# Decay rows by way of memory: turned decay blocks on VectorE instead of TensorE in a one-core hybrid-mixer kernel

## The chip, the cores and the metric

The kernel runs on one core of a Trainium2 chip. The metric is device time in microseconds (us), the median of several executions. Engines are written as the profile writes them: PE is TensorE (PEld its weight load), DVE is VectorE, ACT is ScalarE, POOL is GpSimd and SP is SyncE.

## The reference, cut to what matters

Two blocks run one after the other on 256 tokens of width 2048. The change lies in the first one, in its gated delta rule of 8 heads of width 128:

```python
g = jnp.cumsum(g.reshape(B, H, N, C), axis=-1)
kb = k * beta[..., None]
decay = jnp.exp(jnp.where(incl, g[..., :, None] - g[..., None, :], NEG_INF))
L = jnp.where(strict, jnp.einsum('bhnid,bhnjd->bhnij', kb, k) * decay, 0.0)
T = lax.linalg.triangular_solve(L + eye, jnp.broadcast_to(eye, L.shape), left_side=True, lower=True)
...
intra = jnp.where(incl, jnp.einsum('bhnid,bhnjd->bhnij', q, k) * decay, 0.0)
```

Everything else that fills the time is the dense part around it: `h @ w_in` with more than 12,000 columns, two branch products, `@ w_out`, and the same kind of products of the second block.

## The kernel before, in words

**Pieces.** All dense products are cut into 400 pieces, numbered by ticks 0 to 399. A piece is a 512 KB slab of weights (2 x 128 rows by 512 columns, or 4 x 128 rows by 256 columns). SP loads it into one of five raw buffers (L781), ACT rounds it into a high part `hi_w` (L1002, `split`), DVE computes the remainder `lo_w` (L1406), and PE multiplies with both parts (L2084, L2086, L2094). The split of piece n+2 stands in tick n in the streams of ACT and DVE. There are four split buffers, so ACT may start the high part of piece n as soon as PE has used piece n-4. SP may load into a raw buffer as soon as the low part of the piece five before is done.

**The plan.** `plan()` writes out by hand at which tick every small step stands. Every engine runs through the same list of ticks in order and takes out the steps that are its own. A step that waits for something therefore holds up all that follows it on its engine, the weight splits on ACT and DVE among them. On PE the steps of a tick follow the products of that tick.

**The decay blocks.** Heads are taken in two quads (h = 0, 1) and tokens in two tiles (t = 0, 1). For each of the four (h, t), starting at ticks 65, 69, 73 and 77:

- `gu` (DVE, L1565) multiplies the upper triangle of ones by the log decays, in a high and a low part.
- `gram` (PE): two products with a matrix of ones (L2168) sum these, so that every partition holds the running sum of the decays as a row. Then 8 + 8 products (L2172) form k k^T and k q^T in `aux` banks 1 and 2.
- `decay` (ACT, L1133 and L1136) waits for `gram`, takes the absolute difference of row and column sums, and the exponential.
- `tri` (DVE, L1571 to L1579) masks the decay block below and above the diagonal (`low_m`, `low_t`), forms `attn_t`, and the block `wide` = k k^T times the key factor `k_low` times `low_m`.
- `tri_flip`: PE transposes `wide` (four transposes; in the trace they stand under the helper's line L1973) and ACT copies the result to `low_t` (L1140). The joining steps at ticks 110 to 121 need `low_t`.
- `blocks_away` (POOL, L890) writes the 32x32 diagonal blocks of `wide` to memory for `solve` at tick 83.

`k_scale` on POOL computes `k_low`, `v_shift` on POOL (L900, L901) copies v rows shifted by one to three tokens for the convolution, and `v_tap` on DVE (L1535) reads them. `z_out` on ACT is L1163. POOL's transfers share one queue. `ones_r` (ACT, L1051) makes a rounded copy of the matrix of ones for L2168.

Of the kernel before, what the change touches and what calls it, by code (L numbers as in the profile page):

```python
# [16 lines left out]
F32 = mybir.dt.float32  # L17
F32R = mybir.dt.float32r
# [4 lines left out]
P = 128  # L23
# [183 lines left out]
def plan():  # L207
    steps = [[] for _ in range(TICKS + LAST)]

    def at(tick, *step):  # L210
        steps[tick].append(step)
# [12 lines left out]
    at(18, "ones_r")  # L224
    for n, step in enumerate(("ba", "softplus", "gates", "gcum", "exp_gcum")):
        at(END[("conv", "v", 0, 0)] + 1 + n, step)
    for h in range(2):
        at(conv_end("k", h) + (13, 8)[h], "k_scale", h)

# [21 lines left out]
    for h in range(2):  # L251
        for t in range(NT):
            s = base + 4 * (NT * h + t)
            at(s, "gu", h, t)
            at(s + 1, "gram", h, t)
            at(s + 2, "decay", h, t)
            at(s + 3, "tri", h, t)
            at(s + 5, "tri_flip", h, t)
            at(s + 5, "blocks_away", h, t)
# [181 lines left out]
def build(nc, known, ins, out):  # L441

    ctx = ExitStack()
    with ctx:
# [39 lines left out]
        g_hi = place("g_hi", [P, NT * HEADS], F32R)  # L484
        ones_r = place("ones_r", [P, P], F32R)
# [17 lines left out]
        g_lo = bit(NT * HEADS)  # L503
# [14 lines left out]
        def arena(name, shape, dtype, kb):  # L518
# [14 lines left out]
                  for i, n in enumerate(("low_m", "inv", "wide"))} for t in range(NT)]  # L533
        gu_hi, gu_lo = ([arena(f"gu_{n}{t}", [P, QUAD, P], F32R, 48 + 8 * t + kb) for t in range(NT)]
                        for n, kb in (("hi", 4), ("lo", 2)))
# [36 lines left out]
        for i in range(2):  # L572
# [30 lines left out]
                         for n in ("block", "solved")]  # L603
        scratch = nc.dram_tensor("x2_scratch", [SEQ, D], F32, kind="Internal").ap()
# [31 lines left out]
        v_shifted = {j: signal(f"v_shifted{j}", 16) for j in range(1, CONV)}  # L636
        solved_out = signal("solved_out", 16)
# [205 lines left out]
        def _(pool):  # L843
# [48 lines left out]

            def v_shift(h):

                pool.wait_ge(*act_did.after("v_raw", h, 1))
                pool.wait_ge(*pool_did.after("v_zero", CONV - 1))
                for j in range(1, CONV):
                    if h:
                        pool.wait_ge(*dve_did.after("v_tap", 0, 6))
                    pool.dma_start(v_late[j][j:P], v_late[0][0:P - j]).then_inc(*v_shifted[j].event(h, 0))  # L900
                    pool.dma_start(v_late[j][0:j, 1], v_late[0][P - j:P, 0]).then_inc(*v_shifted[j].event(h, 1))  # L901
# [72 lines left out]
            def tail_(t):  # L974
# [4 lines left out]
                     "solve": solve, "v_shift": v_shift, "inv_zero": inv_zero,  # L979
                     "norm1": norm1, "norm2": norm2, "y_last": y_last, "residual": residual, "att": att, "tail": tail_}  # L980
# [7 lines left out]
        def _(act):  # L988
# [61 lines left out]
            def ones_r_():  # L1050
                act.activation(ones_r[:], ones[:], ACT.Copy).then_inc(*act_did.event("ones_r"))  # L1051

# [26 lines left out]
            def m_out(part, h, s):  # L1079
                c = END[("moba", part, h, s)]  # L1080
                act.wait_ge(*used.after(c))
                if (part, h, s) == ("q", 0, 0):
                    act.wait_ge(*dve_did.after("v_tap", 1, 6))
                act.activation(m_t[part][:, two(h, s)], pairs_of(c)[:, :, 1], ACT.Copy).then_inc(
                    *act_did.event("half", "moba", part, h, s))
# [290 lines left out]
            steps = {"x_flip": x_flip, "sq1": sq1, "ones_r": ones_r_, "softplus": softplus, "exp_gcum": exp_gcum, "sq2": sq2, "split": split, "y_last": y_last, "h2_hi": h2_hi, "h2_rows": h2_rows,  # L1376
                     "raw_out": raw_out, "m_out": m_out, "conv": conv, "conv_silu": conv_silu, "v_raw": v_raw, "v_silu": v_silu,
                     "token_out": token_out, "decay": decay, "tri_flip": tri_flip,
# [15 lines left out]
        def _(dve):  # L1394
# [42 lines left out]
            def gates():  # L1437

                dve.wait_ge(*act_did.after("softplus"))
                link(dve.tensor_scalar(beta, beta, 1.0, None, ALU.add))  # L1440
                link(dve.reciprocal(beta, beta))
                link(dve.tensor_scalar(sp0, sp0, 0.0, None, ALU.max))
                link(dve.tensor_tensor(sp0, sp0, sp1, ALU.add))
                link(dve.tensor_scalar(sp0, sp0, -1.0, None, ALU.mult))
                dve.tensor_tensor(tiles(g, HEADS), tiles(sp0, HEADS), over_heads(nexp, NT), ALU.mult).then_inc(
                    *dve_did.event("g"))
                dve.wait_ge(*dve_did.after("g"))
                link(dve.tensor_copy(g_hi[:], g))
                dve.tensor_tensor(g_lo, g, g_hi[:].bitcast(F32), ALU.subtract).then_inc(*dve_did.event("g_parts"))
# [105 lines left out]
            def gu(h, t):  # L1555
                o = t * HEADS + h * QUAD
                if (h, t) == (0, 0):
                    dve.wait_ge(*dve_did.after("g_parts"))
                    dve.wait_ge(*pe_did.after("conv_back", "k", 1))
                    dve.wait_ge(*act_did.after("silu", "k", 1))  # L1560
                if h:
                    dve.wait_ge(*blocks_out[0][t].after(3))
                    dve.wait_ge(*act_did.after("tri_flip", 0, t))
                for to, part in ((gu_hi[t], g_hi[:].bitcast(F32)), (gu_lo[t], g_lo)):
                    last = dve.tensor_tensor(to[:], over_heads(upto[:]), over_cols(part[:, o:o + QUAD]), ALU.mult)  # L1565
                last.then_inc(*dve_did.event("gu", h, t))

            def tri(h, t):
                c = chain[t]
                dve.wait_ge(*act_did.after("decay", h, t))  # L1570
                dve.tensor_tensor(c["low_m"][:], c["inv"][:], over_heads(below[:]), ALU.mult)  # L1571
                link(dve.tensor_tensor(low_t[h][t][:], c["inv"][:], over_heads(upto[:]), ALU.mult))
                if t == 0:
                    dve.wait_ge(*pool_did.after("k_scale", h))
                dve.tensor_tensor(attn_t[:, quad(h), t], aux[:, 2].rearrange("p (i c) -> p i c", c=P), low_t[h][t][:],
                                  ALU.mult)
                for i in range(QUAD):
                    o = t * HEADS + h * QUAD + i
                    last = dve.scalar_tensor_tensor(c["wide"][:, i], aux[:, 1, i * P:(i + 1) * P], k_low[:, o:o + 1],  # L1579
                                                    c["low_m"][:, i], ALU.mult, ALU.mult)  # L1580
                last.then_inc(*dve_did.event("tri", h, t))

            def lift(h, t):

                inv_q = inv_t[:, quad(h), t]
                if (h, t) == (0, 0):
                    dve.wait_ge(*blocks_back.after(3, NT - 1))
                    for t_ in range(NT):
                        dve.wait_ge(*act_did.after("tri_flip", 1, t_))
# [350 lines left out]
            for no in (1, 2):  # L1940
                x_flip(no)
                for k in range(PIECE_KT):
# [4 lines left out]
                     "token_out": token_out, "v_tap": v_tap, "v_out": v_out, "gu": gu,  # L1947
# [15 lines left out]
        def _(pe):  # L1963
# [448 lines left out]
            def early_products(no):  # L2412
# [17 lines left out]
                if no == 0:  # L2430
# [12 lines left out]
                     "gram": gram, "tri_flip": tri_flip, "pair_y": pair_y, "pair_t": pair_t,  # L2443
# [42 lines left out]
```

## Time and profile before

| what | value |
|---|---|
| time, median of 3 runs | 1200.12 us (1200.05 to 1201.42) |
| profiled execution, its own time | 1200.0 us |
| its span in the trace | 1198.2 us |
| granted TensorE clock | 0.998 |
| PE busy | 1188.3 us (99% of the span) |
| DVE busy | 753.2 us (63%) |
| ACT busy | 609.4 us (51%) |
| POOL busy | 110.8 us (9%) |

The span is the time between the first and the last instruction that the profiler recorded. The device time of the same execution is 1.8 us longer. Busy shares are averages over the whole span. What an edit is worth is decided by the engine that others wait for in that stretch.

### The profile page before, as it was taken

Reading aid. Unit: us, or ns where it says so; the run is one execution under the profiler, and the core shown is the slowest. Engines: PE = TensorE matmul, PEld = TensorE weight load, DVE = VectorE, ACT = ScalarE, POOL = GpSimd, SP = SyncE. Lnnn points to the kernel's source line nnn. Section 1 sums busy time; section 2 is a strip of 40 time slices with the busy share of each in tenths; the row PEclk is TensorE's granted clock in tenths of the full one; section 3 lists DMA queues with packets and bytes.
Section 4 is the critical chain, followed back from the end, with each engine's and each line's share of the span. In section 5 each row is a group of like instructions: output and inputs, shape, how many; then the busy total and the mean of one; then the engine's idle time right before and its main releaser. Section 6 shows DMA issues by size and latency. Waiting matters only on the chain.

```text
span 1198.2 us, 16074 instructions
## 1 busy us (share of the span) xinstructions
PE 1188.3 (99%) x6330; PEld 992.3 (83%) x6330; DVE 753.2 (63%) x990; ACT 609.4 (51%) x895; POOL 110.8 (9%) x149
## 2 busy tenths in 40 slices
PE   9999999999999999999999999999999999999997
PEld 7899888888878888888888888888777778888886
DVE  5776977766575666556455554676665656676654
ACT  6656554644433456534434444574446446555443
POOL 0002020259700110000000000000000000000000
PEclk9999999999999999999999999999999999999999
DMA  8878776566744455555665686566556455454862
GB/s 290 259 207 249 207 198 192 165 207 182 205 135 139 143 163 149 179 187 171 207 192 188 193 293 197 184 199 221 202 187 217 158 193 176 126 156 151 297 195 96
DMA packets 145530, 229.24 MB, mean 191 GB/s; under 512 B 12658, under 2 KB 63538, under 8 KB 144432
## 3 DMA queue, kind: packets, MB, share of 16 engines
q1 hardware_dynamic: 142016, 214.59, 57.7%
q0 software_dynamic: 3120, 12.57, 3.3%
q8 instruction: 50, 0.82, 0.3%
q10 hardware_dynamic: 320, 1.06, 0.2%
q14 instruction: 24, 0.20, 0.0%
HBM read 220.35 MB, written 4.72 MB: 188 GB/s over the span
## 4 chain that ended last, share of the span: by engine, by line
PE 99%; DMA 0%; ACT 0%; DVE 0%; issue 0%; SPq 0%; POOLq 0%; POOL 0%; ACTq 0%
PE acc L2094 69%; PE acc L2084 10%; PE acc L2086 5%; PE aux L1973 4%; PE acc L2035 3%; PE aux L2283 1%; PE aux L2311 1%; PE acc L2425 1%; PE aux L2058 1%; PE aux L2172 1%; PE aux L2276 1%; PE aux L2304 1%; DMA raw_w<-in_w_in 0%; PE aux L2221 0%; PE aux L2213 0%; PE aux L2168 0%
## 5 line engine op out<-in xcount | busy, mean ns | idle before, releaser
L1406 DVE TENSOR_TENSOR lo_w<-raw_w,hi_w 128x1024 fp32r<-128x1024 f32 (+2 forms) x381 | 464.3, 1225 | 327.0 <-ACT hi_w L1002 325.3
L2094 PE MATMUL acc<-hi_w,h_both 128*128 128x512 f32 (+3 forms) x1800 | 559.5, 385 | 0.0
L1002 ACT ACTIVATE hi_w<-raw_w 128x1024 fp32r<-128x1024 f32 (+2 forms) x381 | 394.1, 1049 | 285.9 <-PE acc L2094 185.0
L2094 PEld LDWEIGHTS acc<-hi_w,h_both 128*128 128x128 f32 x1800 | 332.3, 188 | 67.6 <-issue 4.9
L2094 PE MATMUL acc<-lo_w,h_both 128*128 128x512 f32 (+3 forms) x900 | 341.1, 379 | 0.0
L2094 PEld LDWEIGHTS acc<-lo_w,h_both 128*128 128x128 f32 x900 | 169.4, 188 | 28.7
L2084 PE MATMUL acc<-h_both,hi_w 128*128 128x512 f32 x512 | 180.3, 397 | 0.0
L2086 PE MATMUL acc<-h_both,lo_w 128*128 128x256 f32 x512 | 142.9, 279 | 0.0
L2084 PEld LDWEIGHTS acc<-h_both,hi_w 128*128 128x128 f32 x512 | 96.1, 188 | 23.0
L2086 PEld LDWEIGHTS acc<-h_both,lo_w 128*128 128x128 f32 x512 | 96.4, 188 | 0.1
L2094 PE MATMUL acc<-hi_w,m_hi 128*128 128x512 f32 x224 | 87.7, 391 | 0.0
L2094 PE MATMUL acc<-hi_w,m_lo 128*128 128x512 f32 x224 | 87.2, 389 | 0.0
L2094 PE MATMUL acc<-lo_w,m_hi 128*128 128x512 f32 x224 | 87.2, 389 | 0.0
L2094 PEld LDWEIGHTS acc<-hi_w,m_lo 128*128 128x128 f32 x224 | 42.0, 188 | 8.9
L2094 PEld LDWEIGHTS acc<-hi_w,m_hi 128*128 128x128 f32 x224 | 42.1, 188 | 8.6
L2094 PEld LDWEIGHTS acc<-lo_w,m_hi 128*128 128x128 f32 x224 | 42.1, 188 | 8.5
L1193 ACT ACTIVATE att_s<-att_s,small 128x128 f32<-128x128 f32 (+1 forms) x80 | 35.3, 443 | 20.6 <-DVE small L1687 20.6
L1203 ACT ACTIVATE att_p<-aux 128x512 f32<-128x512 f32 (+1 forms) x20 | 16.2, 812 | 35.1 <-PE aux L1973 35.0
L920 POOL TENSOR_TENSOR small_term<-small_block 64x31 f32<-64x31 f32 (+15 forms) x31 | 31.2, 1008 | 2.4
L971 POOL DMA_DIRECT2D x<-x_scratch x1 | 0.8, 767 | 304.4 <-PE aux L2311 304.4
L923 POOL TENSOR_TENSOR small_block<-small_block,small_term 64x31 f32<-64x31 f32 (+15 forms) x31 | 27.3, 879 | 2.4
L860 POOL TENSOR_SCALAR small<-small 128x1 f32<-128x1 f32 (+2 forms) x8 | 3.1, 392 | 246.4 <-DVE small L1919 84.5
(355 smaller groups left out, 1177.8 us busy)
## 6 DMA issues: line engine op xcount, KB each, us to landing
raw_w<-in_w_in SPq DMA_DIRECT2D x275, 512.0 KB, 4.1
raw_w<-in_w_out SPq DMA_DIRECT2D x64, 512.0 KB, 4.7
raw_w<-in_w_branch_a SPq DMA_DIRECT2D x16, 512.0 KB, 4.6
raw_w<-in_w_branch_b SPq DMA_DIRECT2D x16, 512.0 KB, 4.8
raw_w<-in_cmp_k_w SPq DMA_DIRECT2D x8, 512.0 KB, 6.2
raw_w<-in_cmp_v_w SPq DMA_DIRECT2D x8, 512.0 KB, 6.2
raw_w<-in_w_in SPq DMA_DIRECT2D x8, 384.0 KB, 4.6
x_in<-in_x SPq DMA_DIRECT2D x8, 256.0 KB, 7.3
```

Source lines behind the costliest of these rows:

```text
L920: link(pool.tensor_tensor(term, x[:, j + 1:BLOCK, j].unsqueeze(1).broadcast_to([n, rows, cols]), x[:, 0:rows, j].unsqueeze(2).broadcast_to ...
L923: last = pool.tensor_tensor(to, to, term, ALU.add)
L1002: act.activation(piece_flat(hi_w[slot], no), piece_flat(raw_w[no % RAW_SLOTS], no), ACT.Copy).then_inc(*hi_ready.event(no))
L1193: e = act.activation(att_s[:, i * k:(i + 1) * k], att_s[:, i * k:(i + 1) * k], ACT.Exp, bias=nmx[:, i:i + 1], scale=sc, accum_out=den[:, i ...
L1203: act.activation(att_p[:, 0:t + 1], aux[:, b:b + t + 1], ACT.Copy).then_inc(*act_did.event("att_p", kind, h, t))
L1406: dve.tensor_tensor(piece_flat(lo_w[slot], no), piece_flat(raw_w[no % RAW_SLOTS], no), piece_flat(hi_w[slot], no).bitcast(F32), ALU.subtra ...
L1973: return pe.transpose(to, source, ident[0:source.shape[0], 0:source.shape[0]])
L2035: i = pe.matmul(acc[:, g_ % 2, t], x[at], w[:, k], start=first and k == 0 and m == 0, stop=(no, t) in HALF_ENDS and k == n - 1 and m == 2)
L2058: i = pe.matmul(aux[32 * k:32 * (k + 1), 3, 0:256], blk[group.name[1]][:, k0 + k], w[:, k], start=first, stop=last)
L2084: pe.matmul(to[:, c].rearrange("p (b c) -> p b c", b=2), hi[:, k, cols], x, start=first and k == 0, stop=False)
L2086: i = pe.matmul(to[:, c, 0:SEQ], lo[:, k, cols], x[:, 0], start=False, stop=last and k == n - 1)
L2094: i = pe.matmul(to[:, t, 0:group.cols], x[at], w[:, k], start=first and k == 0 and m == 0, stop=last and k == n - 1 and m == 2)
```

## The change

The row of running decay sums is no longer summed by PE. POOL writes the 128 x 16 sums `gcum` to memory turned (`g_rows`, tick 35, right behind the shifted copies of `v_shift` in tick 34), waits for that write in tick 43, and then reads the 2048 numbers back into every partition (`g_rows_back`). The key factors `k_low` go the same way, a quad at a time (`k_rows` at ticks 47 and 59, `k_rows_back` at ticks 54 and 67). `gu`, the two products of L2168, `ones_r` and `tri_flip` are gone. `decay` no longer waits for `gram` and stands one tick earlier. `tri` gets two more DVE products, which make the turned block directly: k k^T (symmetric, from bank 1) times the upper decay block, times the key factors as a row.

```diff
-    at(18, "ones_r")
     for n, step in enumerate(("ba", "softplus", "gates", "gcum", "exp_gcum")):
         at(END[("conv", "v", 0, 0)] + 1 + n, step)
+    at(conv_end("v", 0) + 2, "g_rows")
+    at(conv_end("v", 0) + 10, "g_rows_back")
     for h in range(2):
         at(conv_end("k", h) + (13, 8)[h], "k_scale", h)
+    for h, (away, back) in enumerate(((V_TICKS[0][-1] - 5, V_TICKS[0][-1] + 2), (2, 10))):
+        at(conv_end("v", h) + away, "k_rows", h)
+        at(conv_end("v", h) + back, "k_rows_back", h)
...
-            at(s, "gu", h, t)
             at(s + 1, "gram", h, t)
-            at(s + 2, "decay", h, t)
+            at(s + 1, "decay", h, t)
             at(s + 3, "tri", h, t)
-            at(s + 5, "tri_flip", h, t)
             at(s + 5, "blocks_away", h, t)
...
+            def g_rows():
+
+                pool.wait_ge(*dve_did.after("gcum"))
+                pool.dma_start(g_scratch.rearrange("n p -> p n"), gcum, allow_slow_non_contiguous=True).then_inc(
+                    *g_away.event(0))
+
+            def g_rows_back():
+                pool.wait_ge(*g_away.after(0))
+                pool.dma_start(g_row[:].rearrange("p t h c -> p (t h c)"),
+                               g_scratch.rearrange("n p -> (n p)").partition_broadcast(P)).then_inc(*g_back.event(0))
+
+            def k_rows(h):
+
+                pool.wait_ge(*pool_did.after("k_scale", h))
+                rows = [slice(t * HEADS + h * QUAD, t * HEADS + (h + 1) * QUAD) for t in range(NT)]
+                for t in range(NT):
+                    pool.dma_start(k_scratch[rows[t]].rearrange("n p -> p n"), k_low[:, rows[t]],
+                                   allow_slow_non_contiguous=True).then_inc(*k_away[h].event(t))
+
+            def k_rows_back(h):
+                rows = [slice(t * HEADS + h * QUAD, t * HEADS + (h + 1) * QUAD) for t in range(NT)]
+                pool.wait_ge(*k_away[h].after(NT - 1))
+                pool.wait_ge(*dve_did.after("v_tap", 0, 6))
+                for t in range(NT):
+                    pool.dma_start(k_row[:, t, quad(h)].rearrange("p h c -> p (h c)"),
+                                   k_scratch[rows[t]].rearrange("n p -> (n p)").partition_broadcast(P)).then_inc(
+                        *k_back[h].event(t))
...
                 if (part, h, s) == ("q", 0, 0):
                     act.wait_ge(*dve_did.after("v_tap", 1, 6))
+                    act.wait_ge(*dve_did.after("tri", 1, 1))
...
                 c = chain[t]
-                act.wait_ge(*pe_did.after("gram", h, t))
+                if h:
+                    act.wait_ge(*dve_did.after("tri", 0, t))
+                elif t == 0:
+                    act.wait_ge(*g_back.after(0))
+                    act.wait_ge(*dve_did.after("ssq", "k", 1))
                 for i in range(QUAD):
                     o = t * HEADS + h * QUAD + i
-                    last = act.activation(c["inv"][:, i], aux[:, 0, i * P:(i + 1) * P], ACT.Abs,
+                    last = act.activation(c["inv"][:, i], g_row[:, t, h * QUAD + i], ACT.Abs,
                                           bias=ngcum[:, o:o + 1])
...
-            def tri_flip(h, t):
-                act.wait_ge(*pe_did.after("tri_flip", h, t))
-                act.activation(low_t[h][t][:], aux[:, 3].rearrange("p (i c) -> p i c", c=P), ACT.Copy).then_inc(
-                    *act_did.event("tri_flip", h, t))
...
-                link(dve.tensor_copy(g_hi[:], g))
-                dve.tensor_tensor(g_lo, g, g_hi[:].bitcast(F32), ALU.subtract).then_inc(*dve_did.event("g_parts"))
...
-            def gu(h, t):
-                o = t * HEADS + h * QUAD
...
-                for to, part in ((gu_hi[t], g_hi[:].bitcast(F32)), (gu_lo[t], g_lo)):
-                    last = dve.tensor_tensor(to[:], over_heads(upto[:]), over_cols(part[:, o:o + QUAD]), ALU.mult)
-                last.then_inc(*dve_did.event("gu", h, t))
...
             def tri(h, t):
                 c = chain[t]
                 dve.wait_ge(*act_did.after("decay", h, t))
+                dve.wait_ge(*pe_did.after("gram", h, t))
+                if h:
+                    dve.wait_ge(*blocks_out[0][t].after(3))
+                if t == 0:
+                    dve.wait_ge(*k_back[h].after(NT - 1))
...
                 last.then_inc(*dve_did.event("tri", h, t))
+                dve.wait_ge(*dve_did.after("tri", h, t))
+                link(dve.tensor_tensor(low_t[h][t][:], aux[:, 1].rearrange("p (i c) -> p i c", c=P), low_t[h][t][:],
+                                       ALU.mult))
+                dve.tensor_tensor(low_t[h][t][:], low_t[h][t][:], k_row[:, t, quad(h)],
+                                  ALU.mult).then_inc(*dve_did.event("tri_turned", h, t))
...
             def gram(h, t):
-                take(0, (act_did, "decay", h, t))
-                pe.wait_ge(*act_did.after("ones_r"))
-                take(1, (dve_did, "tri", h, t))
+                take(1, (dve_did, "tri_turned", h, t))
                 take(2, (dve_did, "tri", h, t))
-                pe.wait_ge(*dve_did.after("gu", h, t))
                 for part in "qk":
                     pe.wait_ge(*act_did.after("silu", part, h))
-                for m, part in enumerate((gu_hi[t], gu_lo[t])):
-                    pe.matmul(aux[:, 0], ones_r[:], part[:].rearrange("p i c -> p (i c)"), start=m == 0, stop=m == 1)
...
-            def tri_flip(h, t):
-                take(3, (act_did, "tri_flip", h, t))
-                pe.wait_ge(*dve_did.after("tri", h, t))
-                for i in range(QUAD):
-                    last = turn(aux[:, 3, i * P:(i + 1) * P], chain[t]["wide"][:, i])
-                last.then_inc(*pe_did.event("tri_flip", h, t))
```

## Rows read from the trace of the kernel before

**Rows 1.** The page, part 1: the span and each engine's busy time.

```profile
span 1198.2 us, 16074 instructions
...
PE 1188.3 (99%) x6330; PEld 992.3 (83%) x6330; DVE 753.2 (63%) x990; ACT 609.4 (51%) x895; POOL 110.8 (9%) x149
```

**Rows 2.** The page, part 4: the chain that ended last, shares by engine.

```profile
PE 99%; DMA 0%; ACT 0%; DVE 0%; issue 0%; SPq 0%; POOLq 0%; POOL 0%; ACTq 0%
```

**Rows 3.** PE's waits, longest first: total us, times, longest us.

```profile
PE acc L2410 <- POOL ones L852: 1.1, 1, 1.1
```

**Rows 4.** The same chain in order of time around `gram`: start, us, what.

```profile
196.02 0.46 PE aux L2168 x2
...
209.19 0.44 PE aux L1973 x4
209.63 0.47 PE aux L2168 x2
...
236.83 0.69 PE aux L2168 x2
```

**Rows 5.** DVE groups by shape, 180 to 260 us: busy, mean ns, idle before.

```profile
L1575 DVE TENSOR_TENSOR attn_t<-aux,low_t 128x512 f32<-128x512 f32 x4 | 2.8, 691 | 0.1
L1572 DVE TENSOR_TENSOR low_t<-inv,upto 128x512 f32<-128x512 f32 x4 | 2.7, 684 | 0.0
L1565 DVE TENSOR_TENSOR gu_hi<-upto,g_hi 128x512 fp32r<-128x512 f32 x4 | 2.7, 683 | 0.0
```

**Rows 6.** ACT groups by shape, the same stretch.

```profile
L1136 ACT ACT_TABLE_LOAD x2 | 2.6, 1283 | 0.0
...
L1140 ACT ACTIVATE low_t<-aux 128x512 f32<-128x512 f32 x4 | 2.4, 600 | 18.7 <-PE aux L1973 18.7
```

**Rows 7.** ACT's timeline around the first `decay`: start, us, what, idle before.

```profile
193.34 1.27 ACT L1163 ACTIVATE zs<-acc,small 128x512 f32<-128x512 f32 x2 [1.60 <-PE acc L2094]
194.49 1.06 ACT L1002 ACTIVATE hi_w<-raw_w 128x1024 fp32r<-128x1024 f32 x1
198.30 1.14 ACT L1133 ACTIVATE inv<-aux,small 128x128 f32<-128x128 f32 x4 [2.75 <-PE aux L2172]
```

**Rows 8.** DVE's timeline: the first split behind `tri`.

```profile
206.48 1.21 DVE L1406 TENSOR_TENSOR lo_w<-raw_w,hi_w 128x1024 fp32r<-128x1024 f32 x1
```

**Rows 9.** POOL's timeline: first `k_scale`, and the second `v_shift`.

```profile
108.75 1.26 POOL L882 TENSOR_TENSOR small<-small 128x8 f32<-128x8 f32 x1
...
173.21 0.66 POOL L900 DMA_DIRECT2D v_late<-v_raw  x1 [3.72 <-ACT v_raw L1008]
```

**Rows 10.** The line of `blocks_away`: issue ns min/median/max, and its landings.

```profile
L890 POOL DMA_DIRECT2D block_scratch<-wide x16: 548/550/606, 206.9 to 248.2; - x16
...
DMA to landing us min/median/max: 1.7/3.1/3.6
```

**Rows 11.** POOL's queue, 205 to 252 us: packets, MB, share of 16 engines.

```profile
q0 software_dynamic: 512, 0.26, 2.2%
```

**Rows 12.** The page, part 3: SP's queue over the whole span.

```profile
q1 hardware_dynamic: 142016, 214.59, 57.7%
```

**Rows 13.** Two stretches: us, five engines' busy us, clock, DMA share, GB/s.

```profile
104.00:122.00 18.00, 18.00 (x105) 15.75 (x104) 13.69 (x17) 9.64 (x14) 6.33 (x10) 1.00 1.00 283
122.00:142.00 20.00, 20.00 (x120) 17.56 (x120) 19.29 (x26) 13.14 (x16) 0.00 (x0) 1.00 0.68 197
```

**Rows 14.** Weight loads issued from 104 to 135 us: their landings.

```profile
DMA to landing us min/median/max: 3.5/4.6/10.3
```

**Rows 15.** ACT's timeline: two splits in a row.

```profile
109.26 1.06 ACT L1002 ACTIVATE hi_w<-raw_w 128x1024 fp32r<-128x1024 f32 x1 [1.71 <-PE acc L2086]
112.03 1.06 ACT L1002 ACTIVATE hi_w<-raw_w 128x1024 fp32r<-128x1024 f32 x1 [1.71 <-PE acc L2086]
```

**Rows 16.** DVE's waits, 150 to 260 us: the shifted copies.

```profile
DVE v_late L1535 <- DMA v_late<-v_raw: 1.2, 1, 1.2
```

**Rows 17.** DMA issues: count, KB each, median us to landing.

```profile
v_rows<-in_conv_w SPq DMA_DIRECT2D x8, 256.0 KB, 5.7
...
post_row<-in_post_norm_w POOLq DMA_DIRECT2D x1, 1024.0 KB, 12.0
```

More of the change, by code:

```diff
@@ L483, in build @@
         half = place("half", [P, 16], F32)
-        g_hi = place("g_hi", [P, NT * HEADS], F32R)
-        ones_r = place("ones_r", [P, P], F32R)
         r1_row = place("r1_row", [P, SEQ], F32)
@@ L502, in build @@
         k_v, k_low, k_beg = (bit(NT * HEADS) for _ in range(3))
-        g_lo = bit(NT * HEADS)
         tail, sp0, sp1, nexp = bit(HEADS), bit(NT * HEADS), bit(NT * HEADS), bit(HEADS)
@@ L533, in build @@
                   for i, n in enumerate(("low_m", "inv", "wide"))} for t in range(NT)]
-        gu_hi, gu_lo = ([arena(f"gu_{n}{t}", [P, QUAD, P], F32R, 48 + 8 * t + kb) for t in range(NT)]
-                        for n, kb in (("hi", 4), ("lo", 2)))
+        g_row = arena("g_row", [P, NT, HEADS, P], F32, 100)
+        k_row = arena("k_row", [P, NT, HEADS, P], F32, 64)
         low_t = [[arena(f"low_t{h}{t}", [P, QUAD, P], F32, (54 + 8 * t, 96 + 2 * t)[h]) for t in range(NT)]
@@ L603, in build @@
                          for n in ("block", "solved")]
+        g_scratch, k_scratch = (nc.dram_tensor(f"{n}_row_scratch", [NT * HEADS, P], F32, kind="Internal").ap()
+                                for n in "gk")
         scratch = nc.dram_tensor("x2_scratch", [SEQ, D], F32, kind="Internal").ap()
@@ L636, in build @@
         v_shifted = {j: signal(f"v_shifted{j}", 16) for j in range(1, CONV)}
+        g_away, g_back = signal("g_away", 16), signal("g_back", 16)
+        k_away, k_back = ([signal(f"k_{n}{h}", 16) for h in range(2)] for n in ("away", "back"))
         solved_out = signal("solved_out", 16)
@@ L979, in _ @@
                      "solve": solve, "v_shift": v_shift, "inv_zero": inv_zero,
+                     "g_rows": g_rows, "g_rows_back": g_rows_back, "k_rows": k_rows, "k_rows_back": k_rows_back,
                      "norm1": norm1, "norm2": norm2, "y_last": y_last, "residual": residual, "att": att, "tail": tail_}
@@ L1048, in sq1 @@
                          for c in range(n // 2 * 2, n // 2 * 2 + 2)], ("sq1", n))
-            def ones_r_():
-                act.activation(ones_r[:], ones[:], ACT.Copy).then_inc(*act_did.event("ones_r"))
             def softplus():
@@ L1375, in _ @@
                     early_split(no, k)
-            steps = {"x_flip": x_flip, "sq1": sq1, "ones_r": ones_r_, "softplus": softplus, "exp_gcum": exp_gcum, "sq2": sq2, "split": split, "y_last": y_last, "h2_hi": h2_hi, "h2_rows": h2_rows,
+            steps = {"x_flip": x_flip, "sq1": sq1, "softplus": softplus, "exp_gcum": exp_gcum, "sq2": sq2, "split": split, "y_last": y_last, "h2_hi": h2_hi, "h2_rows": h2_rows,
                      "raw_out": raw_out, "m_out": m_out, "conv": conv, "conv_silu": conv_silu, "v_raw": v_raw, "v_silu": v_silu,
-                     "token_out": token_out, "decay": decay, "tri_flip": tri_flip,
+                     "token_out": token_out, "decay": decay,
                      "delta": delta, "delta_norm": delta_norm, "z_out": z_out,
@@ L1446, in gates @@
                     *dve_did.event("g"))
-                dve.wait_ge(*dve_did.after("g"))
-                link(dve.tensor_copy(g_hi[:], g))
-                dve.tensor_tensor(g_lo, g, g_hi[:].bitcast(F32), ALU.subtract).then_inc(*dve_did.event("g_parts"))
             def gcum_():
@@ L1553, in token_out @@
                 dve.tensor_reduce(tiles(to, QUAD), sq[:], AXX, ALU.add).then_inc(*dve_did.event("ssq", part, h))
-            def gu(h, t):
-                o = t * HEADS + h * QUAD
[L1557 to L1563, printed above, removed]
-                for to, part in ((gu_hi[t], g_hi[:].bitcast(F32)), (gu_lo[t], g_lo)):
-                    last = dve.tensor_tensor(to[:], over_heads(upto[:]), over_cols(part[:, o:o + QUAD]), ALU.mult)
-                last.then_inc(*dve_did.event("gu", h, t))
             def tri(h, t):
@@ L1586, in lift @@
                 if (h, t) == (0, 0):
+                    dve.wait_ge(*dve_did.after("tri_turned", 1, 1))
                     dve.wait_ge(*blocks_back.after(3, NT - 1))
-                    for t_ in range(NT):
-                        dve.wait_ge(*act_did.after("tri_flip", 1, t_))
                 link(dve.tensor_tensor(inv_q, inv_q, over_heads(upto[:]), ALU.mult))
@@ L1946, in _ @@
                      "gcum": gcum_, "r1_row": r1_row_, "raw_out": raw_out, "m_out": m_out, "conv": conv,
-                     "token_out": token_out, "v_tap": v_tap, "v_out": v_out, "gu": gu,
+                     "token_out": token_out, "v_tap": v_tap, "v_out": v_out,
                      "tri": tri, "lift": lift, "pair_y": pair_y, "pair_t": pair_t,
@@ L2442, in _ @@
                      "conv_back": conv_back, "h2_flip": h2_flip, "norm2_col": norm2_col_,
-                     "gram": gram, "tri_flip": tri_flip, "pair_y": pair_y, "pair_t": pair_t,
+                     "gram": gram, "pair_y": pair_y, "pair_t": pair_t,
                      "join_y": join_y, "join_t": join_t, "delta": delta,
```

## The prediction

> **What bounds the kernel now.** I read the page first. PE is busy 99% of a span of 1198.2 us, DVE 63% and ACT 51% [rows 1], and the chain that ended last is PE for 99% [rows 2]. Busy time of a pipelined engine can flatter it, so I looked at PE's waits next: the longest in the whole program is 1.1 us, at the start [rows 3], and none stands near the decay blocks. So PE is the bound in every stretch that the change touches. The sum is then simple: what leaves PE's stream is gained in full, what moves to DVE, ACT, POOL or DMA costs nothing until PE is kept waiting. Both halves need numbers.
>
> **What leaves PE.** The chain in order of time gives exclusive time, while one product's duration overlaps its neighbours, so I take the chain. Four `tri_flip` steps of four transposes take 0.44 us each [rows 4]; the other three, at 222.81, 236.40 and 250.33, read the same. That is 4 x 0.44 = 1.76 us. The pairs of L2168 take 0.46, 0.47, 0.47 (at 223.24, not shown) and 0.69 us [rows 4], together 2.09 us. The last holds about 0.2 us of lost issue that need not vanish with it, so the pairs are worth 1.85 to 2.1 us. Sum: 3.6 to 3.85 us. I take 3.85, since the lost issue stands between the two things removed. The 16 products of L2172 stay.
>
> **DVE.** Removed are eight products of L1565 (0.68 us) and two tiny ones. Added are eight of the same size: four read a PSUM bank, as L1575 does (0.69 us), four read SBUF only, as L1572 does (0.68 us) [rows 5]. The total is unchanged within 0.1 us. What changes is the place: one `tri` grows by 2 x 0.69 = 1.4 us in one block. The split behind the first `tri` now starts at 206.48 [rows 8]. `tri` itself can begin earlier, because `decay` waits no more for `gram`: ACT sat idle 2.75 us before it at 198.30 [rows 7]. ACT then reaches the split ahead of `tri` some 2 us earlier, against 1.4 us of longer `tri`, which leaves the splits no later than now. The new waits inside `tri` have the following splits queued behind them, and PE behind those. `gram` of the next tile also waits now for the end of the longer `tri`, which stands two ticks before it; by the above that ends near 206 us, and `gram` comes after tick 70, near 209 us [rows 4]. I take 0 for DVE. If the gain of an early `decay` failed, the 1.4 us would lie inside PE's lead, which is worked out below at 6 us.
>
> **ACT.** Removed are four copies of 0.60 us, before which ACT idled 18.7 us in total [rows 6], and one copy of ones. Added are probably two table loads of 1.28 us [rows 6]: in tick 66 `decay` (Exp) now comes ahead of `z_out` (Silu), where before `z_out` ran at 193.34 with no load and `decay` came after it [rows 7]. In that tick ACT then does 1.28 + 1.14 + 0.63 us of decay, 1.28 us of table and 1.27 us of `z_out`. The next split slips from 194.49 to about 198. PE takes that piece at about 203 (tick 69: two pieces of 2.7 us and one `gram` behind 196.0), so some 3 us of cover remain, after the 1.22 us of its low part. I take 0, and 2 us as the worst.
>
> **POOL and the row traffic.** What the trace does not show is a turned write. The layout makes each number a run of 4 bytes: 2048 runs for `gcum`, 4 x 512 = 2048 for `k_low`. The nearest rows are those of `blocks_away`: 16 writes of 128 runs of 128 bytes, to memory, on the same queue. They are issued in 0.55 us each and land in 1.7 to 3.6 us [rows 10]. From 205 to 252 us this queue moved just these 2048 runs and took 2.2% of 16 engines [rows 11]: 0.022 x 16 x 47 = 16.5 us, or 8 ns a run. By that all 4096 new runs take 33 us of engine time, 2 us spread over 16. The other end is a full weight packet: 0.577 x 16 x 1198 us / 142016 = 78 ns [rows 12]. By that the 2048 runs of `g_rows` occupy all 16 engines for 10 us, and a k quad for 5 us. I take the lower, being the same kind of write; both ends stay in the range. Issuing may take 0.55 us (one row) up to 16 times that, 8.8 us, for 2048 runs; behind it on POOL wait only `k_scale` (108.75 [rows 9]), whose reader `v_out` stands twenty ticks later, and later `token_out`.
>
> The reads back are one of 1024 KB and four of 256 KB. Like rows landed in 12.0 and 5.7 us [rows 17]. The 2 MB are 1% of the 229 MB that the page gives.
>
> Their deadlines: `g_rows` is issued near 109 us, `g_rows_back` near 130 us, and `decay` needs the row near 192 us, so 60 us of cover. `k_rows` 0 goes at about 141 us, its read at 160 us, `tri` needs it at 200 us. `k_rows` 1 goes at 177 us, its read at 199 us, and is needed near 229 us. Each `..._back` step waits on POOL for its write: 21, 19 and 22 us after it. All are many times 3.1 us.
>
> The Trainium skill speaks against this change. Its page "DMA: Bandwidth & Descriptors", section "Rules for kernel authors", says that a strided last dimension costs one descriptor per element, and that turning by a plain rearranged access pattern is 19 times as slow as the hardware transpose. No run here shows either form of turning yet. The factor put on the 3.1 us landing would be, as an estimate from that page, 59 us a write; where it would lead stands beside the second rival.
>
> **How late weights may come.** The dangerous place is 104 to 122 us, where the shifted copies already fill the DMA engines (share 1.00 [rows 13]) and weight loads land after up to 10.3 us instead of 4.6 [rows 14]. PE still didn't wait. ACT starts a high part when PE has used the piece four before, three pieces ahead of use. Splits follow each other by 2.77 us there (112.03 - 109.26 [rows 15]). So 3 x 2.77 - 1.06 - 1.22 = 6.0 us are left. `g_rows` stands behind the shifted copies in the same queue, so its runs prolong this crowded stretch: by 1 us at 8 ns a run, by 10 us at 78 ns.
>
> **Sum.** The sum is made against the profiled execution: 1198.2 us of span and 1.8 us around it, 1200.0. The median, 1200.12, is 0.1 us above it. 1200.12 - 3.85 + 0 = 1196.3 us. From no change this differs by 0.32%; a measurement of this kernel tells about 0.2% (2.4 us).
>
> **Rival 1, no measurable change (0.18).** The weights come late behind `g_rows`, or ACT's crowded tick 66 and the longer `tri` add up, and PE waits 1.5 to 6 us. For: the DMA engines are full there, DVE is busy 19.29 of the 20 us that follow [rows 13] and repairs a delay slowly. Against: 6 us of cover, and 8 ns by the nearest row. At 78 ns a run, 10 - 6 = 4 us of waiting eat the gain: 1200.3 us. The whole case covers 1197.8 to 1202.5.
>
> **Rival 2, slower (0.12).** The turned writes are slow enough to hold POOL's queue. The second `v_shift` (173.21 [rows 9]) now stands behind `k_rows_back` 0, which waits for the write of `k_rows` 0 issued at 141 us, and before that for `g_rows`. DVE already waits 1.2 us for these copies [rows 16], so each us of delay reaches DVE, and PE after the 6 us of cover. With a k write that lands after T us, `v_shift` comes T - 32 us late (173 - 141 = 32) and PE waits T - 32 - 6 us, if the write of `g_rows` is hidden. The case begins at T = 38 and costs net time from T = 38 + 3.85 = 42 us. A write of 50 us gives 1196.3 + 12 = 1208 us, which I take as its time. Against it speak landings of 3.6 us at most [rows 10], and that T stays under 12 us even if issuing and moving cost the upper bounds of a quad (2.2 + 5 us) on top of that.
>
> By the rule of the Trainium skill's page "DMA: Bandwidth & Descriptors" (section "Rules for kernel authors") this rival is the case: at the estimate of 59 us `g_rows` would hold `k_rows` 0 until 168, its write would land at 227, `v_shift` would come 54 us late, and the time would be about 1196 + 54 - 6 = 1244 us.
>
> **Rival 3, the change does not do it on PE (0.02).** Weight loads of PE may be the true pacing item and the gaps simply move. PEld is busy 83%, so I give it almost nothing; the time would be 1200.1.
>
> **Numbers.** The forecast, faster by more than 2.4 us, has 0.68, and its own range is 1195.7 to 1197.7: 0.6 us of additional semaphore waits saved below, up to 1.4 us of small waits above. The cases of no measurable change have 0.18 + 0.02 = 0.20, slower has 0.12. For 8 in 10 the range takes the forecast and most of rival 1, up to its centre at 1200.3 and a little more: 1195.5 to 1200.8. It leaves out rival 2 and rival 1's upper edge.
>
> **What would show it.** In the trace of after: PE instructions fewer by 24 and no L2168 or transposes of `wide`; the chain still 99% PE; PE's waits near 110 to 130 and 195 to 215 us absent (a row there names rival 1, with its price). The landings of the two turned writes decide between 8 and 78 ns, and rival 2: under 20 us, POOL never waits long in the `..._back` steps; weight loads near 110 us landing above 16 us would mean that the cover is gone. ACT should show two more table loads, DVE the same total. Wrong it would be made by a PE wait that I placed nowhere, such as one on the new `tri_turned` event in `gram`.

## The result, and the profile after

| kernel | median | span of the profiled execution | its own time |
|---|---|---|---|
| before | 1199.97 us (6 runs; 1200.12 in the 3 shown ahead) | 1198.2 us | 1200.0 us |
| after | 1204.47 us (6 runs, 1203.86 to 1206.78) | 1202.0 us | 1203.86 us |

The ratio is 1.0040, 95% interval 1.0029 to 1.0051: the change made the kernel 4.5 us slower. I had forecast 3.85 us faster.

The page after, parts 1 and 4: the answers to [rows 1] and [rows 2].

```profile
span 1202.0 us, 16028 instructions
...
PE 1187.1 (99%) x6306; PEld 990.8 (82%) x6306; DVE 754.3 (63%) x988; ACT 610.2 (51%) x892; POOL 117.8 (10%) x159
...
PE 96%; DMA 2%; DVE 1%; ACT 0%; SPq 0%; issue 0%; POOLq 0%; POOL 0%; ACTq 0%
```

PE has exactly 24 instructions fewer, and its busy time did not grow. DVE's total is 1.1 us larger, where eight products were swapped for eight and I had expected 0.1 us at most. But the chain is no longer PE alone: 3% of it are DMA and DVE. Most of those 3% are one place, which the chain in order of time shows from 120 to 165 us (start, us, what):

```profile
117.78 22.54 DMA raw_w<-in_w_in
...
140.34 1.06 ACT hi_w L1034
...
141.42 1.24 DVE lo_w L1435
```

A weight load issued at 117.78 took 22.5 us to land, then came its high part, its low part, and only then PE. That is the chain for which the prediction gave 6 us of cover. The waits after say the same; the first line is PE's, the answer to [rows 3], the second ACT's from 60 to 300 us.

```profile
PE acc L2106 <- DVE lo_w L1435: 5.6, 2, 4.8
```

```profile
ACT hi_w L1034 <- DMA raw_w<-in_w_in: 23.6, 8, 6.6
```

The stretch in slices of 4 us (us, busy us of PE, PEld, DVE, ACT, POOL, granted clock, DMA share, GB/s) shows the course:

```profile
112.00:116.00 4.00, 4.00 (x25) 3.48 (x25) 1.99 (x3) 2.35 (x3) 0.00 (x0) 1.00 1.04 266
116.00:120.00 4.00, 4.00 (x25) 3.52 (x24) 3.93 (x8) 1.85 (x4) 0.00 (x0) 1.00 1.50 174
120.00:124.00 4.00, 4.00 (x25) 3.48 (x24) 2.63 (x3) 0.24 (x1) 0.00 (x0) 1.00 1.11 79
124.00:128.00 4.00, 4.00 (x25) 3.52 (x24) 0.06 (x1) 1.06 (x1) 1.00 (x2) 1.00 0.79 84
128.00:132.00 4.00, 3.18 (x18) 2.52 (x17) 4.00 (x4) 2.59 (x3) 1.15 (x2) 1.00 1.07 386
132.00:136.00 4.00, 4.00 (x24) 3.45 (x23) 3.89 (x8) 0.91 (x2) 0.00 (x0) 1.00 1.30 267
136.00:140.00 4.00, 1.97 (x12) 1.45 (x10) 0.51 (x2) 0.00 (x0) 0.00 (x0) 1.00 0.94 101
140.00:144.00 4.00, 1.21 (x4) 1.05 (x5) 2.58 (x3) 2.61 (x3) 0.00 (x0) 0.88 0.82 197
144.00:148.00 4.00, 4.00 (x21) 3.53 (x21) 3.22 (x4) 3.99 (x5) 0.00 (x0) 0.69 0.94 285
```

The slices from 120 to 128 us in the kernel before:

```profile
120.00:124.00 4.00, 4.00 (x25) 3.52 (x24) 4.00 (x6) 1.94 (x2) 0.00 (x0) 1.00 0.85 272
124.00:128.00 4.00, 4.00 (x25) 3.48 (x24) 3.71 (x5) 1.81 (x4) 0.00 (x0) 1.00 0.79 229
```

Twice the DMA engines are busy (a share of 0.79 to 1.11; the view can put it above 1) and move little: 79 to 84 GB/s from 120 to 128 us, where before moved 272 and 229, and 101 GB/s from 136 to 140. After each of these valleys PE stands: 0.82 us missing at 128 to 132, then 2.03 + 2.79 us at 136 to 144. Behind the second pause the granted clock is 0.88 and 0.69, that is partly the lower of its two levels (1.2 instead of 2.4 GHz; slices of 1 us read 0.50 to 0.52 from 143 to 146 us, when PE was at work again). This costs (0.12 + 0.31) x 4 = 1.7 us of work. In all 5.64 + 1.7 = 7.3 us are lost, against 3.85 gained.

What filled the DMA engines stands in POOL's timeline, the answer to [rows 9]:

```profile
108.52 1.24 POOL L899 DMA_DIRECT2D g_row_scratch<-small  x1
...
126.99 0.62 POOL L904 DMA_DIRECT2D g_row<-g_row_scratch  x1 [15.18 <-DMA g_row_scratch<-small]
127.62 1.54 POOL L912 DMA_DIRECT2D k_row_scratch<-small  x2
```

The turned write of the sums landed 18.2 us after its issue (the line of DMA issues), and the weight loads issued from 100 to 135 us landed late:

```profile
g_row_scratch<-small POOLq DMA_DIRECT2D x1, 8.0 KB, 18.2
```

```profile
DMA to landing us min/median/max: 3.9/14.2/22.5
```

The first valley ends when the turned write of the sums lands (126.99). The 1 MB read and the turned write of the key factors start at once after it, and the second valley follows. Around `gram`, the place that the change meant to relieve, all is as hoped. In the chain of after, only the products of L2189 (L2172 of before) are left there; [rows 4] answer to this. The first and last of the four:

```profile
203.74 1.78 PE aux L2189 x16
...
241.78 1.78 PE aux L2189 x16
```

### The profile page after: what moved, and what is told of

It reads as the page before. It is cut to its first block, busy times and chain, and to the rows that moved or that the text cites. A ratio compares the mean times of both kernels' runs of the same rounds, so it can differ in the third digit from the quotient of the medians.

```text
span 1202.0 us, 16028 instructions
## 1 busy us (share of the span) xinstructions
PE 1187.1 (99%) x6306; PEld 990.8 (82%) x6306; DVE 754.3 (63%) x988; ACT 610.2 (51%) x892; POOL 117.8 (10%) x159
## 4 chain that ended last, share of the span: by engine, by line
PE 96%; DMA 2%; DVE 1%; ACT 0%; SPq 0%; issue 0%; POOLq 0%; POOL 0%; ACTq 0%
PE acc L2116 69%; PE acc L2106 9%; PE acc L2108 4%; PE aux L1995 3%; PE acc L2057 3%; DMA raw_w<-in_w_in 2%; PE aux L2293 1%; PE aux L2321 1%; PE aux L2080 1%; PE aux L2189 1%; PE acc L2435 1%; PE aux L2286 1%; PE aux L2314 1%; DMA x_in<-in_x 0%; PE aux L2231 0%; PE aux L2223 0%
```

## The experiments

Theory A: the short runs of the turned writes hold up the weight loads, each at a fixed price. Rival B: the transfers follow one another too closely. Rival C: it is the 2 MB of reads. The medians of before on the chips of these runs were 1199.74 us (e1 to e4), 1199.8 us (e5 to e8) and 1199.67 us (e9 to e11).

| run | median us | ratio to before, 95% |
|---|---|---|
| e1_whole | 1195.89 | 0.9970 (0.9958 to 0.9981) |
| e2_g_whole | 1197.25 | 0.9980 (0.9971 to 0.9989) |
| e3_k_whole | 1197.76 | 0.9982 (0.9972 to 0.9991) |
| e4_apart | 1202.38 | 1.0031 (1.0015 to 1.0048) |
| e5_write1 | 1200.62 | 1.0007 (0.9997 to 1.0016) |
| e6_write2 | 1210.66 | 1.0080 (1.0056 to 1.0104) |
| e7_pad2 | 1214.10 | 1.0120 (1.0104 to 1.0135) |
| e8_read | 1199.63 | 0.9997 (0.9988 to 1.0007) |
| e9_sums_only | 1198.47 | 0.9992 (0.9982 to 1.0002) |
| e10_turn_only | 1204.03 | 1.0038 (1.0023 to 1.0053) |
| e11_whole_again | 1195.90 | 0.9968 (0.9957 to 0.9979) |

**e1_whole: the same change with whole runs.** Instead of turning on the way out, the numbers are written as they lie and picked with a step on the way in.

```diff
-        g_row = arena("g_row", [P, NT, HEADS, P], F32, 100)
-        k_row = arena("k_row", [P, NT, HEADS, P], F32, 64)
+        g_row = arena("g_row", [P, P, NT * HEADS], F32, 100)
+        k_row = arena("k_row", [P, NT, 2, P, QUAD], F32, 64)
...
-                pool.dma_start(g_scratch.rearrange("n p -> p n"), gcum, allow_slow_non_contiguous=True).then_inc(
-                    *g_away.event(0))
+                pool.dma_start(g_scratch, gcum).then_inc(*g_away.event(0))
...
-                    pool.dma_start(k_scratch[rows[t]].rearrange("n p -> p n"), k_low[:, rows[t]],
-                                   allow_slow_non_contiguous=True).then_inc(*k_away[h].event(t))
+                    pool.dma_start(k_scratch[t, h], k_low[:, rows[t]]).then_inc(*k_away[h].event(t))
...
-                    last = act.activation(c["inv"][:, i], g_row[:, t, h * QUAD + i], ACT.Abs,
+                    last = act.activation(c["inv"][:, i], g_row[:, :, o], ACT.Abs,
...
-                dve.tensor_tensor(low_t[h][t][:], low_t[h][t][:], k_row[:, t, quad(h)],
+                dve.tensor_tensor(low_t[h][t][:], low_t[h][t][:], k_row[:, t, h].rearrange("p c i -> p i c"),
```

> The kernel after, but the sums and the key factors are written as they lie (128 runs of 64 bytes, and 4 times 128 runs of 16 bytes, instead of 4096 runs of 4 bytes) and read back in that order; ACT and DVE pick their row with a step of 16 or 4 numbers. Bytes, reads, waits and PE's work are those of after. Theory A (the many 4-byte runs hold up the weight loads): PE never waits, and the 3.85 us of removed PE work appear in full, 1196.2 us. Theory B (the transfers come too close behind one another, whatever their runs): the 1 MB read still follows the shifted copies, so part of the loss stays, 1198 to 1202 us. Theory C (the 2 MB of reads are what costs): as after, 1204 us. If picking with a step were slow on ACT or DVE, their groups L1167 and L1603 would be longer than 0.38 and 0.69 us, which PE's cover should hide.

Measured 1195.89 us and, in the repetition e11, 1195.90. That is 3.85 and 3.77 us less than before (the interval of e1 is 2.3 to 5.0 us), and 8.6 us less than after. This is theory A's number, and below B's 1198 to 1202 us. The write of the sums and its read landed after 8.8 and 7.8 us (min and max of the tile's landings):

```profile
DMA to landing us min/median/max: 7.8/8.3/8.8
```

The same write took 18.2 us in after. The 8.8 us are for the most part waiting behind the shifted copies, the last of which land at about 117 us in both kernels, so the 2048 short runs cost 18.2 - 8.8 = 9.4 us. Weight loads from 100 to 135 us landed as in [rows 14], where after had a median of 14.2 and a maximum of 22.5:

```profile
DMA to landing us min/median/max: 3.5/5.0/10.4
```

Picking with a step is not free. ACT's 16 instructions grew from 0.39 to 0.51 us and DVE's four from 0.69 to 1.08 us; the third line shows the table loads of `decay`:

```profile
L1165 ACT ACTIVATE inv<-g_row,small 128x128 f32<-128x128 f32 x16 | 7.0, 512 | 0.0
L1601 DVE TENSOR_TENSOR low_t<-low_t,k_row 128x512 f32<-128x512 f32 x4 | 4.3, 1083 | 0.1
L1168 ACT ACT_TABLE_LOAD x3 | 3.8, 1283 | 0.1
```

Both are hidden: PE's only wait is the one at the start. Theory C falls, since all 2 MB of reads are in this kernel.

**e2_g_whole and e3_k_whole: one of the two writes each in whole runs.**

```diff
# e2: only the lines of g_scratch and g_row above; k_rows still turned
# e3: only the lines of k_scratch and k_row above; g_rows still turned
```

> Only the sums are written in whole runs of 64 bytes; the key factors are still written turned, in 4-byte runs. After showed PE waits of 0.8 us near 131 us and 4.8 us near 139 us. Theory A: 1024 short runs are left in the crowded stretch, half of those of the sums, so weight loads land late by about 5 us, inside 6 us of cover: 1196 to 1198 us. Theory B: about the same, since without the slow first write nothing piles up. Theory C: 1204 us.

> Only the key factors are written in whole runs of 16 bytes; the sums are still written turned. Theory A: the first starved stretch stays (weight loads landing after 16 to 22 us, a wait of about 1 us on PE), the second goes: 1197 to 1199 us. Theory B: the 1 MB read still comes right behind the slow write and the late weight loads, so most of the 4.8 us wait stays: 1201 to 1204 us. Theory C: 1204 us.

Measured 1197.25 and 1197.76 us. By the medians the turned key factors alone cost 1.4 us against e1, the turned sums alone 1.9 us, and both together 8.6 us. The two don't add: about 5.3 us appear only where both are there. A's ranges hold for both runs. B's range for e3 (1201 to 1204 us) does not: the 1 MB read still starts right behind the slow write, at 125.78 us, and PE's wait for weights is 1.0 us, not 4.8. But a fixed loss of PE time for each write, which is how A's price is put here, falls too, since the losses don't add. What remains is a price that each write takes from the loads, and a cost to PE that depends on what it still finds of the cover.

The slower of a quad's two writes landed after 11.6 us (quad 0) and 14.9 us (quad 1) in e2, where they are turned, and after 6.9 and 8.5 us in e1, in whole runs. That is 4.7 and 6.4 us for 1024 runs. Quad 0 stands behind the 1 MB read, quad 1 behind the second set of shifted copies.

**e4_apart: the same turned writes, spaced.**

```diff
                 pool.wait_ge(*g_away.after(0))
+                pool.wait_ge(*dve_did.after("v_tap", 0, 3))
...
                 pool.wait_ge(*pool_did.after("k_scale", h))
+                if h == 0:
+                    pool.wait_ge(*dve_did.after("ssq", "q", 1))
```

> The kernel after with the same transfers, all in their 4-byte form, but spaced: the read of the sums waits on POOL for the fourth v_tap product (about 135 us), and the first write of key factors for DVE's sums of squares of the second q (about 144 us or later) instead of following at once at 127.6 us. Theory A alone, each write costing its own delay whatever its neighbours: still two starved stretches, 1202 to 1205 us. Theory B: each starved stretch alone fits into PE's cover or nearly, 1197 to 1200 us.

Measured 1202.38 us (1200.75 to 1207.76), within A's numbers and above B's 1197 to 1200 us, but not for A's reason. In the place where after lost 5.6 us, PE now lost next to nothing (19.99 of 20 us busy from 122 to 142), and the write at 149.58 starved the loads from 152 to 160 us (68 and 41 GB/s) without a wait on PE either. The loss came later. The chain from 110 to 200 us:

```profile
179.95 15.43 DMA v_late<-v_raw
...
195.40 1.23 DVE v_late L1564
```

The second set of shifted copies started 4 us later than in before (177.23 against 173.21), with the turned write of quad 1 behind it. It landed after 15.4 us, where before had 10.1. The write behind it does not explain this, since after has the same order and also 10.1 us. The weight loads issued from 176 to 184 us were slower too (median 12.2 us to landing, 4.6 in after and 8.6 in before). Why just this place was so crowded is not shown; that the loads were still catching up is my guess. DVE stood 9.8 us before it and PE then 3.9 us, followed by a lower clock (0.89 and 0.69 in the slices from 196 to 204 us, 1.7 us of work). So spacing does help the first two writes, and B is right there. But the loss was not gone, it came at the next crowded place.

**e5 to e8: one kind of transfer at a time, added to the kernel before.** One turned write, two of them, two that aren't turned, and one read.

```diff
+    at(conv_end("v", 0) + 2, "g_rows")
...
+            def g_rows():
+
+                pool.wait_ge(*dve_did.after("gcum"))
+                for m in range(2):                    # e5: range(1)
+                    pool.dma_start(g_scratch[m].rearrange("n p -> p n"), gcum, allow_slow_non_contiguous=True).then_inc(
+                        *g_away.event(m))
# e7: the destination is g_scratch[m, :, :, 0] of a [2, P, NT * HEADS, 2] scratch
# e8: instead of the writes, behind v_tap 0 1:
+                pool.dma_start(g_row[:], ins["post_norm_w"][0].partition_broadcast(P)).then_inc(*g_away.event(0))
```

> The kernel before with one thing added: the 128 x 16 sums are written to memory turned (2048 runs of 4 bytes) right behind the shifted copies. Nobody reads them. PE's work is unchanged. The runs of the kernel after and of its mends put this write at 18.2 us to landing against 8.8 us for the same bytes in whole runs, so 9.4 us of nearly stopped weight loads, against about 8 us of cover. Theory A: 1200.5 to 1202 us, weight loads landing after up to 18 to 22 us. If the loss of after needs its reads as well: 1199.7 us.

> The same with the turned write made twice, one behind the other (4096 runs). Theory A, a fixed price of about 73 ns per run on each of 16 engines: another 9.4 us of stopped loads with no cover left, so PE waits about 10 us, and loses up to 2 us more to a lower clock after the wait: 1210 to 1213 us. If the price were one of issuing or of landing, not of runs, hardly more than with one write: 1202 us.

> As the run with two writes, with the same 4096 runs of 4 bytes, but not turned: each number goes to every second place of a row, 8 bytes from its neighbour instead of 512. If the number of runs is what costs, 1210 to 1213 us as with the two turned writes. If the turned addresses cost, each run in another stretch of memory, clearly less: 1200 to 1204 us.

> The kernel before with one 1 MB read added, a row of 2048 numbers into all 128 partitions, issued behind the first shifted product (about 123 us). No turned write. Theory A: the read is 4 or more packets a partition of full size, weight loads land a few us later, PE doesn't wait: 1199.7 us. Theory C (reads cost): 1203 us or more.

Measured 1200.62, 1210.66, 1214.10 and 1199.63 us. The first difference is not clear of zero by its interval, though the profile has the wait. e7 lies above its expected 1210 to 1213 us, the others fit theirs. PE's waits in e5 and e6:

```profile
PE acc L2096 <- DVE lo_w L1418: 1.5, 1, 1.5
```

```profile
PE acc L2096 <- DVE lo_w L1418: 9.7, 1, 9.7
```

One write of 2048 runs landed after 18.4 us, as in after, and used up the cover: by estimate 9.4 - 1.5 = 7.9 us of it, where I had estimated 6. The second went straight through to PE, 8.2 us of waiting more, and a lower clock behind it (0.50 from 136 to 140 us, 0.59 from 140 to 144), 10.0 us in the median. Landings of the writes in e6, then in e7:

```profile
DMA to landing us min/median/max: 18.3/21.3/24.4
```

```profile
DMA to landing us min/median/max: 20.5/24.8/29.0
```

In e6 the second write, issued 1.3 us after the first, landed 109.6 + 24.4 = 134.0 against 108.3 + 18.3 = 126.6: 7.4 us for 2048 runs. In e7 it is 138.5 - 128.9 = 9.6 us. If the runs are spread evenly over 16 engines (128 each), these are 58 and 75 ns a run. The first write gives 9.4 / 128 = 73 ns in after and (20.5 - 8.8) / 128 = 91 ns in e7, the key factors of e2 4.7 / 64 = 73 ns and 6.4 / 64 = 100 ns. All are estimates from landings. The runs of e7 lie 8 bytes apart instead of 512 and cost no less. So turned addresses are not what costs. The same bytes in fewer and longer runs are cheap (e1), so it is the cutting into 4-byte runs. Why such a run takes this long is not shown. That e7 is 3.4 us slower than e6 is hardly waiting (10.1 against 9.7 us in the two profiles); its clock is below 1.00 in five slices of 4 us from 128 to 148 us, that of e6 in three. The read of 1 MB alone costs nothing. It landed after 6.0 us and left 144 records, about one for a partition, not the four or more that I had expected.

**e9_sums_only and e10_turn_only: the halves of the change, with whole runs.**

```diff
# e9: from e1; k_rows and the two added DVE products out, tri_flip back on PE and ACT
# e10: from before; tri_flip out, k_rows and the two DVE products in; gu now waits
-                    dve.wait_ge(*act_did.after("tri_flip", 0, t))
+                    dve.wait_ge(*dve_did.after("tri_turned", 0, t))
```

> Half of the change with whole runs: only the decay sums come from memory, PE still turns the blocks (tri_flip stays, no key rows). The chain of before gives the pairs of L2168 1.85 to 2.09 us, so 1199.7 - 2.0 = 1197.7 us.

> The other half with whole runs: PE still sums the decays (gu, L2168), and DVE turns the blocks with key rows from memory. The chain of before gives the transposes 1.76 us, so 1199.7 - 1.8 = 1197.9 us. DVE now has both gu and the two added products in each tile, 2.4 us more per tile than in either kernel; if its splits were near the limit, PE would wait and the gain would be smaller.

> The mended kernel of the first call once more beside its two halves, on the same chip: 1195.9 us, and the gains of the halves should add up to its gain of 3.85 us within 0.4 us.

Measured 1198.47, 1204.03 and 1195.90 us. The first half brings 1.2 us by the median (expected 2.0; the interval is -0.2 to 2.2 us, so the gain is not clear of zero). The second costs 4.4 us where I expected 1.8 us of gain. The halves give -3.2 us and the whole 3.77, so the expectation that they add up within 0.4 us failed. PE's waits in e10, and DVE's timeline at the second tile:

```profile
PE aux L2191 <- DVE gu_lo L1583: 4.5, 3, 1.9
```

```profile
206.38 1.08 DVE L1604 TENSOR_TENSOR low_t<-low_t,k_row 128x512 f32<-128x512 f32 x1
207.37 1.22 DVE L1424 TENSOR_TENSOR lo_w<-raw_w,hi_w 128x1024 fp32r<-128x1024 f32 x1
208.50 0.69 DVE L1583 TENSOR_TENSOR gu_hi<-upto,g_hi 128x512 fp32r<-128x512 f32 x1
209.10 0.69 DVE L1583 TENSOR_TENSOR gu_lo<-upto,small 128x512 fp32r<-128x512 f32 x1
```

With the sums still on PE, the longer `tri` pushes `gu` back, and `gram` waits for `gu`, three times by up to 1.9 us. In the whole change this wait is not there (e1), and the other half both takes `gu` out of DVE's stream and frees `decay` from `gram`. Which of the two makes the turning on DVE free is not shown. That this is the whole of the 4.4 us is not shown: the waits are 4.5 us against 1.76 us saved, which makes 2.7 us of the profiled execution's 2.7 (1202.41 against 1199.67), while the median lies 1.6 us higher.

## Why the prediction was wrong

**The step that failed** is the price of a turned run. The prediction put it between 8 and 78 ns, took the lower value, "being the same kind of write", and got 1 us of crowding for `g_rows`. Measured are 58 to 100 ns, most of them near the upper bound, and 9.4 us of crowding. The lower bound came from packet records [rows 11]. But such records don't price short runs: e5 has 3168 records on POOL's queue where before has 3120, that is 48 more for 2048 runs:

```profile
q0 software_dynamic: 3168, 12.58, 3.3%
```

[rows 11] itself has 512 packets for what I counted as 2048 runs. The landings [rows 10] could not exclude the upper bound either, as 128 runs are 8 for each engine, 0.6 us at 73 ns, inside the spread of 1.7 to 3.6 us. I had compared durations at a count where the term could not show.

**The second failed step** is the timing of POOL. I set the transfers at their ticks: read of the sums near 130 us, key factors at 141. But a tick paces an engine only through its waits, and POOL has few. `k_rows` 0 went at 127.6, right behind the read of the sums, and met the backlog of the first write. Rival 1 treated `g_rows` alone; e3 shows that this would have cost less than the gain (1.9 us).

**Cover.** Six us was somewhat low (7.9 by e5). I noted that DVE "repairs a delay slowly", but used the cover as if it were full for each write. It is used once: in after, DVE ran without a gap from the first late load (127.94) until it stood for the second (136.5 to 141.42).

**The clock.** No term of the sum had it. It cost 1.7 us in after, all of it behind the long pause.

**What held.** 3.85 us for PE: e1 measured 3.85 and 3.77. The match to the second digit is luck, given an interval of 2.3 to 5.0 us. The longer `tri` and the new wait of `gram` on `tri_turned` cost nothing in after and e1 (0.2 us in e2). ACT: two more table loads, as said (`decay` has three instead of two, and `zs` now has one), hidden. Issuing: 1.24 us for 2048 runs, near the low end. Reads: 12.5 and 5.8 us to landing against 12.0 and 5.7 foreseen, and free (e8). The sign of rival 1 came as written: weight loads issued from 108 to 112 us landed after 17.4 and 18.2 us, above 16. It had the right mechanism and, at 78 ns a run, the right size for `g_rows` (10 us). PE's 5.64 us of waiting even lie in its 1.5 to 6 us, but it counted one write and no clock, was centred at 1200.3, and ended short of 1204.5. (Its upper edge adds up to 1196.3 + 6 = 1202.3, not 1202.5.) Rival 2 did not come: it needed a quad's write of 38 us, and the longest write of all took 18.2. The bound of "under 12 us" for a quad was too low, 13.8 us in after, and its 2.2 us of issuing were those of one of the two writes. `v_shift` was 8 us late (180.92) for another reason, since PE and all behind it had slipped by as much.

The account of after against e1, both by span: 1194.0 + 5.64 + 1.7 = 1201.3 against 1202.0; 0.7 us stay unassigned.

The Trainium skill's page "DMA: Bandwidth & Descriptors" says in "Rules for kernel authors" that a strided last dimension costs one descriptor per element. By that rule the number of elements costs, not where they go, and e7 agrees. Its factor of 19 compares turning by access pattern with the hardware transpose, which no run here has, so the factor is not tested. The prediction had put it on the 3.1 us of another kind of write; the resulting estimate of 59 us is three times the 18.2 us that were measured. Against the same bytes in whole runs the turned write landed after 18.2 instead of 8.8 us, both with the same queue ahead of them.

## What to carry to other kernels

Price a transfer by its contiguous runs as well as by its bytes: by estimate about 75 ns per 4-byte run and engine here (58 to 100 ns), during which the weight loads behind it fall to about a third of their rate (79 to 84 against 229 to 272 GB/s). If a turn can be made by the reader's step instead of by the writer's runs, take that: the same 3.85 us of PE work then came out as gain, and e1 beats both kernels. And when several delays draw on one cushion, ask what refills it between them.

## What I had not expected of the hardware

Busy DMA engines don't mean moved data: from 120 to 128 us their share was 0.79 to 1.11 while the rate was 79 to 84 GB/s, and 8 KB of numbers in 4-byte runs was all that stood in the way. The short runs leave almost no records of their own (48 for 2048 runs). From 118 to 127 us the weight queue has 657 records and 99% of 16 engines, 217 ns for each record, where the whole run before has 78. The price of reading with a step, 16 numbers apart on ACT, was 0.39 to 0.51 us, and 4 numbers apart on DVE 0.69 to 1.08 us.
